# Attention heads of a two-layer backbone: late transposes inside the keys products, conversions moved within the rounds, probabilities scaled on GpSimd

## What is computed

```python
kvu = (ckv @ w_ukv)                       # 8 heads of 128 key and 128 value columns, from 256 latents
k_nope, v = kvu[..., :NOPE_DIM], kvu[..., NOPE_DIM:]
s = (einsum('bqhd,bkhd->bhqk', qn_b, k_nope)
     + einsum('bqhr,bkr->bhqk', qr_b, k_rope))
p = softmax(s.astype(float32) * ATTN_SCALE, axis=-1)
o = einsum('bhqk,bkhd->bqhd', p, v)       # then o @ w_o
```

## Time and profile before

| | |
|---|---|
| median of 3 runs | 3479.03 us (3474.29 to 3485.82) |
| the profiled execution | 3489.05 us, span 3487.1 us |
| TensorE busy | 3246.7 us of the span |
| VectorE, ScalarE, GpSimd busy | 1782.4, 956.1, 164.2 us |
| the heads, from the first maxima to the last products | about 1946 to 2561 us of the span |
| share of TensorE in the chain that ended last | 79% |

### The profile page before, as it was taken

How to read it: one execution, slowest core, us unless ns; L and a number is a source line. 1 busy time by engine, 2 the same in 40 slices (tenths; PEclk the granted TensorE clock), 3 DMA queues, 4 the chain that set the end, 5 groups by cost and what they waited for, 6 DMA issues and landing times.

```text
span 3487.1 us, 48061 instructions
## 1 busy us (share of the span) xinstructions
PE 3246.7 (93%) x18847; PEld 3149.3 (90%) x18847; DVE 1782.4 (51%) x3001; ACT 956.1 (27%) x1337; POOL 164.2 (5%) x201
## 2 busy tenths in 40 slices
PE   6999999998999999999779789898869999999997
PEld 4999999997999999999779678888769999999996
DVE  8666888786333333334635555555544333333333
ACT  4333212124111111112312554554623111111114
POOL 3000000003000000001200000000000000000002
PEclk8999999998999999999889899999989999999998
DMA  6444433320111111111103100101001111111111
GB/s 213 136 153 141 119 102 105 105 91 29 38 46 43 41 39 44 40 42 46 43 23 128 57 30 17 33 14 38 13 12 31 43 42 42 42 42 42 42 42 61
DMA packets 272667, 210.25 MB, mean 60 GB/s; under 512 B 15102, under 2 KB 243756, under 8 KB 272572
## 3 DMA queue, kind: packets, MB, share of 16 engines
q1 hardware_dynamic: 260908, 163.50, 15.4%
q0 software_dynamic: 11664, 45.39, 3.7%
HBM read 185.10 MB, written 23.76 MB: 60 GB/s over the span
## 4 chain that ended last, share of the span: by engine, by line
PE 79%; DVE 12%; issue 4%; ACT 3%; DMA 1%; SPq 0%; POOL 0%; DVEq 0%; ACTq 0%; POOLq 0%
PE set L559 65%; PE set L1049 4%; PE set L1037 3%; PE turned L802 2%; DVE pa L2211 2%; DVE soft L2670 2%; PE set L636 1%; DVE tmp L2028 1%; DVE hlo L2037 1%; PE set L702 1%; DVE pah L2152 1%; DVE x L2005 1%; PE set L593 1%; PE turned L733 1%; DVE ptl L2685 1%
## 5 line engine op out<-in xcount | busy, mean ns | idle before, releaser
L559 PE MATMUL set<-hhi,whi 128*128 128x384 f32 x2856 | 660.6, 339 | 8.2 <-DVE wlo L1922 6.1
L559 PE MATMUL set<-hlo,whi 128*128 128x384 f32 x2856 | 655.3, 337 | 0.0
L559 PE MATMUL set<-hhi,wlo 128*128 128x384 f32 x2856 | 655.1, 337 | 0.0
L2229 DVE SCALAR_TENSOR_TENSOR x<-set,mod,x 128x128 f32<-128x128 f32 x744 | 413.2, 612 | 279.4 <-PE set L559 279.1
L559 PEld LDWEIGHTS set<-hhi,whi 128*128 128x128 f32 x2856 | 512.9, 190 | 9.1 <-issue 6.7
L559 PEld LDWEIGHTS set<-hlo,whi 128*128 128x128 f32 x2856 | 515.3, 190 | 0.0
L559 PEld LDWEIGHTS set<-hhi,wlo 128*128 128x128 f32 x2856 | 515.3, 190 | 0.0
L1922 DVE TENSOR_TENSOR wlo<-wraw,whi 128x1024 fp32r<-128x1024 f32 x193 | 235.5, 1221 | 464.6 <-ACT whi L1183 434.9
L1183 ACT ACTIVATE whi<-wraw 128x1024 fp32r<-128x1024 f32 (+1 forms) x207 | 214.1, 1035 | 657.0 <-PE set L559 654.2
L1183 ACT ACTIVATE tmp<-set 128x1152 f32<-128x1152 f32 x97 | 110.1, 1135 | 712.9 <-PE set L559 704.4
L559 PE MATMUL set<-ghi,whi 128*128 128x384 f32 x1296 | 294.9, 335 | 1.6 <-DVE x L2229 1.6
(11 more groups left out here) (238 smaller groups left out, 4182.1 us busy)
## 6 DMA issues: line engine op xcount, KB each, us to landing
wraw<-in_f_w_in SPq DMA_DIRECT2D x176, 256.0 KB, 3.0
adu<-in_ada_w SPq DMA_DIRECT2D x48, 512.0 KB, 6.0
wraw<-in_f_w_out SPq DMA_DIRECT2D x88, 256.0 KB, 3.1
wraw<-in_a_w_in SPq DMA_DIRECT2D x64, 256.0 KB, 3.1
v_scratch<-vst POOLq DMA_DIRECT2D x16, 576.0 KB, 3.0
vld<-v_scratch POOLq DMA_DIRECT2D x16, 576.0 KB, 4.5
q_scratch<-tmp POOLq DMA_DIRECT2D x16, 576.0 KB, 3.2
aldr<-in_ada_w SPq DMA_DIRECT2D x8, 1024.0 KB, 11.1
```

What stands on the lines that cost most here:

```text
L559: last = nc.tensor.matmul(ps[:, b, 0:cols], w, m[:, b * cols:(b + 1) * cols], start=(i == 0 and p == 0), stop=(i == n - 1 and p == 2))
L2229: last = v.scalar_tensor_tensor(dst, src, k.mod[:, gate + n, c:c + 1], dst, ALU.mult, ALU.add)
```

## The change

It does three things.

- **Late transposes in the keys job.** On TensorE, slot 6's first two groups are turned ahead of the keys job, and its last group between the two halves of that job. ScalarE takes slot 6's first groups before the exponentials of slot 8 and the last one behind them, VectorE before and behind the inverse sum of slot 8; both did it after the query and key conversions.
- **Conversions within the rounds.** A new method `between` stands in rounds 2 and 5 (queries, when there is a next head) and 3 and 4 (weights, in odd heads). On ScalarE it comes behind the first groups of the round and ahead of its exponentials, on VectorE at the round's end. In odd heads `o_split` moves from behind slot 1's exponentials to ahead of slot 0's (ScalarE) and from the end to behind slot 0's inverse sum (VectorE).
- **Scaling on GpSimd.** `normalise` is gone from ScalarE; GpSimd multiplies each slot's probabilities by the inverse sums and counts up `p_ready`. `inverse_sum` waits for the scaling of two slots before. The loads of the queries stand in GpSimd's stream behind the nine slots of a head.

The diff, without `last_head`'s and the start's repeats:

```diff
@@ -999,7 +999,7 @@
 
     KEY_CH = ((0, 480), (480, 944), (944, KEYS))
 
-    def keys_job(self, h):
+    def keys_job(self, h, late=None, off=0):
 
         k, nc, s = self.k, self.nc, KV_SLOT
         ps = self.open()
@@ -1009,6 +1009,8 @@
                 for b, (lo, hi) in enumerate(self.KEY_CH):
                     last = nc.tensor.matmul(ps[:, b, 0:hi - lo], w, m[:, n, lo:hi],
                                             start=(n == 0 and p == 0), stop=(n == CT - 1 and p == 2))
+            if n == 0 and late is not None:
+                self.turn_probs(late, True, off)
         self.close(last)
 
     def values_job(self, blocks):
@@ -1109,9 +1111,8 @@
         self.head_middle(h)
         if h == 1:
             self.unit_ready()
-        self.keys_job(1 - h)
         self.turn_probs(6, False, 1)
-        self.turn_probs(6, True, 1)
+        self.keys_job(1 - h, 6, 1)
         self.weighted_job(h, 2)
         self.turn_probs(7, False, 2)
         self.next_head_ready()
@@ -1713,34 +1714,35 @@
         if before:
             self.read_out(1 - h, 3)
 
-    def head_round(self, h, s, pair=-1):
+    def between(self, h, s, ahead):
+
+        if ahead and s in (2, 5):
+            self.queries_hi(s // 3)
+        if h == 1 and s in (3, 4):
+            self.kv_split(s - 3) if ahead else self.split()
+
+    def head_round(self, h, s, ahead, pair=-1):
 
         if pair != -1:
             self.eng.wait_ge(self.k.mm_done, self.J.at(1))
         self.turned(s, False)
+        self.between(h, s, ahead)
         self.exponentials(s + 2, 3)
         if pair != -1:
             self.read_out(h, pair)
         self.turned(s, True)
-        self.normalise(s + 2, 3)
         self.B.step()
 
     def head_middle(self, h, ahead):
 
-        self.head_round(h, 1)
-        if ahead:
-            self.queries_hi(0)
-        self.head_round(h, 2, 0)
-        if h == 1:
-            self.kv_split(0) if ahead else self.split()
-        self.head_round(h, 3, None)
-        if h == 1:
-            self.kv_split(1) if ahead else self.split()
-        self.head_round(h, 4)
-        if ahead:
-            self.queries_hi(1)
-        self.head_round(h, 5, 1)
+        self.head_round(h, 1, ahead)
+        self.head_round(h, 2, ahead, 0)
+        self.head_round(h, 3, ahead, None)
+        self.head_round(h, 4, ahead)
+        self.head_round(h, 5, ahead, 1)
+        self.turned(6, False)
         self.exponentials(8, 3)
+        self.turned(6, True)
 
     def weighted_read(self, h, pair):
 
@@ -1754,30 +1756,22 @@
         self.head_middle(h, True)
         self.queries_hi(2)
         self.keys_hi()
-        self.turned(6, False)
-        self.turned(6, True)
-        self.normalise(8, 3)
         self.B.step()
         self.weighted_read(h, 2)
         self.turned(7, False)
         self.turned(7, True)
         self.turned(8, False)
+        if h == 1:
+            self.o_split()
         self.exponentials(0, 3)
-        self.normalise(0, 3)
         self.B.step()
         self.turned(8, True)
         self.exponentials(1, 3)
-        self.normalise(1, 3)
         self.B.step()
-        if h == 1:
-            self.o_split()
...
@@ -1848,13 +1837,6 @@
         self.act(k.pr[s % 3][:, 0:n], src, ACT.Exp, bias=k.soft[:, 0, q:q + 1], scale=SCALE,
                  accum_out=k.soft[:, 1, q:q + 1]).then_inc(k.freed[self.J.odd()], 1)
         self.J.step()
-
-    def normalise(self, s, off):
-        k, q = self.k, self.B.odd(off - 1)
-        n = CTX if s == CTX_AT else SMP + PAST
-        self.eng.wait_ge(k.inv_ready, self.B.at(off))
-        self.act(k.pr[s % 3][:, 0:n], k.pr[s % 3][:, 0:n], scale=k.soft[:, 2, q:q + 1]
-                 ).then_inc(k.p_ready, 1)
 
     def turned(self, s, rest):
 
@@ -2550,7 +2532,14 @@
         if before:
             self.out_lo(1 - h, 3)
 
-    def head_round(self, h, s, pair=-1):
+    def between(self, h, s, ahead):
+
+        if ahead and s in (2, 5):
+            self.queries_lo(s // 3)
+        if h == 1 and s in (3, 4):
+            self.kv_split(s - 3) if ahead else self.split()
+
+    def head_round(self, h, s, ahead, pair=-1):
 
         self.maxima(s + 2, 3, 0 if pair == -1 else CTX if pair is None else 2 * P)
         self.turned(s, False)
@@ -2558,25 +2547,20 @@
         if pair != -1:
             self.out_lo(h, pair)
         self.turned(s, True)
+        self.between(h, s, ahead)
         self.B.step()
 
     def head_middle(self, h, ahead):
 
-        self.head_round(h, 1)
-        if ahead:
-            self.queries_lo(0)
-        self.head_round(h, 2, 0)
-        if h == 1:
-            self.kv_split(0) if ahead else self.split()
-        self.head_round(h, 3, None)
-        if h == 1:
-            self.kv_split(1) if ahead else self.split()
-        self.head_round(h, 4)
-        if ahead:
-            self.queries_lo(1)
-        self.head_round(h, 5, 1)
+        self.head_round(h, 1, ahead)
+        self.head_round(h, 2, ahead, 0)
+        self.head_round(h, 3, ahead, None)
+        self.head_round(h, 4, ahead)
+        self.head_round(h, 5, ahead, 1)
         self.maxima(8, 3, 0)
+        self.turned(6, False)
         self.inverse_sum(3)
+        self.turned(6, True)
 
     def weighted_read(self, h, pair):
 
@@ -2674,6 +2654,8 @@
     def inverse_sum(self, off):
         k, q = self.k, self.B.odd(off - 1)
         self.eng.wait_ge(k.freed[self.J.odd(-1)], self.J.half(-1) + 1)
+        if self.B.past(0) or off > 2:
+            self.eng.wait_ge(k.p_ready, self.B.at(off - 2))
         self.nc.vector.reciprocal(k.soft[:, 2, q:q + 1], k.soft[:, 1, q:q + 1]).then_inc(k.inv_ready, 1)
 
     def turned(self, s, rest):
@@ -2724,6 +2706,23 @@
                             ).then_inc(k.xr_ready, 1)
         self.T.step(3)
         self.N += 1
+
+    def queries(self, h):
+
+        k, g = self.k, self.eng
+        for b in range(BANKS):
+            g.dma_start(k.qld[b][:], k.q_dram[h, 0, :, b * CH:(b + 1) * CH]).then_inc(k.q_loaded, 16)
+        g.dma_start(k.qlr[:], k.q_dram[h, 1]).then_inc(k.q_loaded, 16)
+
+    def probabilities(self):
+
+        k, g = self.k, self.eng
+        for s in range(9):
+            n, q = CTX if s == CTX_AT else SMP + PAST, self.B.odd()
+            g.wait_ge(k.inv_ready, self.B.at(1))
+            g.tensor_scalar(k.pr[s % 3][:, 0:n], k.pr[s % 3][:, 0:n], k.soft[:, 2, q:q + 1], None, ALU.mult
+                            ).then_inc(k.p_ready, 1)
+            self.B.step()
 
     def program(self):
         k, g, J, T, d = self.k, self.eng, self.J, self.T, self.k.d
@@ -2794,15 +2793,14 @@
         self.G.n = 0
         for n in range(4):
             g.wait_ge(k.q_spilled[n], 16 * (HEADS // 2))
-        for b in range(BANKS):
-            g.dma_start(k.qld[b][:], k.q_dram[0, 0, :, b * CH:(b + 1) * CH]).then_inc(k.q_loaded, 16)
-        g.dma_start(k.qlr[:], k.q_dram[0, 1]).then_inc(k.q_loaded, 16)
-        with repeat(g, HEADS - 1) as i:
-            g.wait_ge(k.q_ready, i + 1)
-            for b in range(BANKS):
-                g.dma_start(k.qld[b][:], k.q_dram[i + 1, 0, :, b * CH:(b + 1) * CH]
-                            ).then_inc(k.q_loaded, 16)
-            g.dma_start(k.qlr[:], k.q_dram[i + 1, 1]).then_inc(k.q_loaded, 16)
+        self.queries(0)
+        g.wait_ge(k.q_ready, 1)
+        self.queries(1)
+        for h in range(HEADS):
+            self.probabilities()
+            if h < HEADS - 2:
+                g.wait_ge(k.q_ready, h + 2)
+                self.queries(h + 2)
         T.step(50 * (HEADS // 2))
         for t in range(2):
             self.third_sums(t, 1, DT)
```

More of the change, by code:

```diff
@@ L1801, in heads @@
             self.exponentials(s, s + 1)
-            self.normalise(s, s + 1)
         self.head_first(0, False)
         self.turned(0, True)
-        self.normalise(2, 3)
         self.B.step()
```

## The result

The changed kernel takes **3503.75 us** (median of 5 runs, 3498.20 to 3506.23) against 3480.71 us (5 runs, 3474.29 to 3485.82) of the kernel before on the same chip: ratio **1.0064** [1.0047, 1.008], 22 us slower. The forecast was 13 us faster. The profiled execution's span is 3504.5 us, 17.4 above that of before.

What follows compares the result with a forecast made beforehand. TensorE, busy 93% of the span, was taken as the bound, leaving its idle time and low clock to win: 45 us gained, less 26 for GpSimd collisions and 6 for clock, makes 13; median about 3466 us, range 3436 to 3496.

Steps and rivals of the forecast that it cites:

- What GpSimd costs: GpSimd scalings of 128x1280, taken as 1.65 us each, hold out VectorE's two-SBUF-input work: 26 us given back.
- Rival 1: GpSimd is slow and rounds 2 and 5 wait for it; at 3.3 us a scaling, 3500 us; chance 0.18.
- The formula: Collision cost over all heads: 17g − 1.75 us, with g the time of one GpSimd scaling.
- the 26 us: Collision of VectorE with GpSimd over all heads: even 3.0, odd 4.1, last about 2 us, given back from the gain.
- Keys section, gain 5.0 and 4.35: End of pair-1 to end of pair-2 products: 5.0 us less in even heads, 4.35 in odd, about 2 the clock.
- The odd head's grows by 0.6: TensorE's wait for slot 8's last copy in odd heads grows 0.6 us, as `o_split` replaces slot 0's normalising pass.
- Round 3, 0.77 becomes 1.9: Even head's round 3: `queries_lo(0)`, moved before the late maximum, lengthens TensorE's wait from 0.77 to 1.9 us.
- Latency covered, 1.1 ahead with 3.3; start-up pays g − 1.36 once: Slot 4's scaling is ready 1.1 us before its transposes even at 3.3 us; only start-up pays scaling time g less 1.36.
- The wait of 2.93 left the clock up: Odd head's round 3 in the kernel before: a 2.93-us TensorE wait did not halve the clock, while 3.92 did.
- `ol` well above 0.42: Sign of being right: VectorE's `ol` in rounds 2 and 5 takes well above 0.42 us beside running scalings.
- Rival 2: Nothing collides, since VectorE gets in first or GpSimd holds the port briefly: 45 us gained, 3434; chance 0.12.
- Rival 3: Late transposes don't hold the clock; keys-job waits and every head's round 3 halve it: 3486 us; chance 0.20.

Runs made afterwards that it cites:

- e3: The changed kernel with scaling taken back to ScalarE, keeping late transposes and all moved conversions: 3438.7 us, ratio 0.9883 to the kernel before.
- e6: The changed kernel with GpSimd scaling only the first 640 of 1280 columns and ScalarE the other 640: 3444.83 us, ratio 0.9898 to the kernel before.
- e1: The kernel before with only the late transposes in the keys job; scaling on ScalarE, conversions in their old places: 3434.43 us, ratio 0.9865.
- e12: The kernel before with late transposes and GpSimd's scaling, all conversions in their old places: 3438.8 us, ratio 0.9881.
- e5: The changed kernel with each reciprocal, which lets GpSimd start, behind its round's conversions on VectorE: 3433.68 us, ratio 0.9854 to the kernel before.
- e9: The changed kernel with each reciprocal last in its round and ScalarE scaling instead of GpSimd: 3453.72 us, ratio 0.9917 to the kernel before.

## Why the prediction was wrong

**The step that failed** is in "What GpSimd costs": "I take 1.65, because reading is what the two share", with 3.3 as the bound from above. The pass of 128x1280 takes 3.52 us undisturbed and 3.67 on the mean, above the bound. Both came from the two-input form, the bound in proportion to the columns written and the 1.65 in proportion to the columns read; the one-input form is no cheaper per column written. The Trainium skill (GPSIMD Engine Reference, Engine selection) has one-input work at roughly line rate; 3.52 us against the estimate of 1.07 say otherwise for this form, a scale taken from a tensor, in fp32.

**With the measured duration the prediction's own sum comes out, in part by luck.** Rival 1 is what happened: 45 − (17 × 3.52 − 1.75) − 12 = −25, measured −22 in the ratio. The fixed part is right: e3 gave 41 us with ScalarE's pass still there, and of the 45 some 4 were that pass, 0.95 in each even head. But the terms of what GpSimd costs are off against each other. The stretches of the changed kernel and e3 differ by 36 us of idle time and 29 of lower clock. The products' waits for low halves, 10.8 us in e3, are 5.3 in the changed kernel, since the pass that stood before slot 8's last copy is gone; so the holds themselves cost some 42 us of idle time. The formula has 58 and 12. A blocked conversion loses 2.7 us in round 2 and 2.55 in round 5, not 3.4, since VectorE is let in before the pass ends and stands some way into it; and the clock falls behind the keys' stop as well as behind round 3's, as the rival said it might. That is the second term that was too small: 6 us for the clock, for round 3 in half of the heads, where all 14 stops of the 7 heads halved it.

**At other durations the formula is wrong.** It charges g in 17 places; with 640 columns (1.89 us) it gives 30 us, and e6 measured 0.9898 − 0.9883, 5 us, with intervals that overlap. So had the pass been 1.65 us long, the 26 us would, by e6, hardly have fallen due, and the kernel would have gone faster than forecast; no run has 1280 columns at that duration. The rule taken from the Trainium skill (SBUF — State Buffer, the section on the two sides of SBUF), that the pair of ports is held for the whole instruction, is contradicted by the three meetings above, as far as the profile's spans of GpSimd go: 0.67 us of 1.90, 0.94 of 2.70, 2.94 of 3.53. The rows from which the prediction took it, of GpSimd's two-input add, have 0.85 of 1.00.

Point by point:
- *Keys section, gain 5.0 and 4.35*: right for e3, where it takes 14.2 us in both heads, 5.3 and 4.7 less than before; one wait of 0.90 us stood there where 1.0 and 1.2 were worked out, and the clock held. In the changed kernel the wait is 3.45, and the clock falls.
- *Slot 0's 0.96 gone*: right. *The odd head's grows by 0.6*: wrong, 1.01 in the changed kernel and 1.02 before; it is 1.54 in e3, where `o_split` and ScalarE's pass both stand there. *Round 3, 0.77 becomes 1.9*: 1.91 in e3; the odd head's 2.93 became 2.00.
- *Latency covered, 1.1 ahead with 3.3; start-up pays g − 1.36 once*: right, TensorE waits for GpSimd only at the start, 3.05 us where it waited 0.82 for ScalarE. *The new wait in `inverse_sum`, nothing*: 1.57 us at the end of each of the three odd heads in the loop.
- *The wait of 2.93 left the clock up*: rightly read, but it didn't carry over; in e1 the same stop halves it, and in e3 a stop of 2.0 does so in two of seven heads.
- *`o_split` goes first*: right, 1220 ns as before.
- *`ol` well above 0.42*: wrong, 428 ns. VectorE's instruction follows the reciprocal before GpSimd has been released; it is the second or third behind it that is held, and `qnl` and `qrp` rose as forecast.
- *The cost of the collision hangs on place*: the prediction listed the places for the changed kernel rightly (rounds 2, 3 and 5), and didn't ask what each would cost where the conversions had stood. e12 shows 6 us net for holds of the same length.
- Rival 2 (nothing collides, 3434) is not what the change did, and its number is what its own instructions give in another order: e5, 3433.68. Rival 3 falls: without GpSimd's scaling the clock holds in the keys job (0.98 over the heads of e3).

Open: why GpSimd holds VectorE out for 2.94 us of 1280 columns and only 0.94 of 960. The pairing of GpSimd with the moves but without the late transposes wasn't tried. That it is the queries' conversions that make the holds dear is read from where the stops lie, rounds 3 and the keys; no run with GpSimd in the changed kernel's order moves them back alone.

## What to carry to other kernels

Work on an engine that can hold another out is priced in two steps: how long the other is held, and what stands behind the held instruction there. With the late transposes in place, holds of the same 2.7 us cost 6 us net over all heads where VectorE would have waited anyway, and 63 where a late maximum stood behind them. So order the queue: put every instruction that can be held ahead of the signal that lets the other engine start, and leave behind it those that read PSUM; or cut the other engine's instruction short. And a long pass can pay on a queue in which nothing waits behind it, even if that engine takes 2.6 times as long (3.52 against 1.36 us): with the reciprocal last it gave 22 us (e9 and e5).

## What the hardware showed that was not expected

- GpSimd's `tensor_scalar`, one fp32 input and a scale from a tensor: 0.60 us for 128 columns, 1.89 for 640, 2.70 for 960, 3.52 for 1280: 2.5 ns a column. Its two-input add of 384 took 1.00 us, so one input less makes it no cheaper per column.
- A VectorE instruction with two SBUF inputs is kept out for less than GpSimd's instruction lasts, and not in proportion to it: it begins to move 0.67 us into a pass of 640 columns, 0.94 into one of 960, 2.94 into one of 1280, and loses at most 0.27 us to pieces of 320.
- VectorE wins where its instructions follow one another: GpSimd's pass is 4.16 us where two of them stood before it.
- A stop of 3.45 us behind a busy stretch was enough for 3.4 to 6.8 us of half clock, in every head. Shorter ones went either way: 2.93 us left the clock up in the kernel before and halved it for some 3.4 us in e1; in e3 2.0 us did so in two heads of seven (0.50 from 2414.8 to 2418.2), and its clock over the heads is 0.98.
